# Products of constant tables on TensorE in six waits of a six-layer fp32 model block

## What is computed

```python
for layer in range(2):
    h = rms_norm(x, mix_pre_g[layer])
    m = mixer_ab(h, ...) if layer == 0 else mixer_cd(h, positions, ...)
    x = x + rms_norm(m, mix_post_g[layer])
    h = rms_norm(x, ffn_pre_g[layer])
    x = x + rms_norm(channel_mixer(h, ...), ffn_post_g[layer])
for l in range(2):
    x = hybrid_layer(x, l, ...)      # projections, four attention groups, output projection
return rms_norm_2(x, final_norm_g)
```

## Time and profile before

| | |
|---|---|
| median of 3 runs | 2828.29 us (2823.17 to 2831.08) |
| the profiled execution | 2837.55 us, span of the core 2835.7 us |
| mean granted TensorE clock | 0.99 |
| TensorE busy | 2749.1 us, 97% |
| VectorE, ScalarE, GpSimd busy | 1945.8 us (69%), 1379.4 us (49%), 518.3 us (18%) |
| read from HBM | 477.25 MB, 169 GB/s over the span |

### The profile page before, as it was taken

One profiled execution on the slowest core, in us unless ns is written; L12 is line 12 of the kernel. 1 busy time (PEld: TensorE's weight loads), 2 busy tenths in 40 slices (PEclk: granted clock), 3 DMA queues, 4 the chain that ended last, 5 costly groups with the idle time before them and its releaser, 6 DMA issues.

```text
span 2835.7 us, 50169 instructions
## 1 busy us (share of the span) xinstructions
PE 2749.1 (97%) x18314; PEld 2484.2 (88%) x18314; DVE 1945.8 (69%) x2757; ACT 1379.4 (49%) x1931; POOL 518.3 (18%) x487
## 2 busy tenths in 40 slices
PE   8999999999999999999999999999999999999998
PEld 8998988888888899988888888899878889987887
DVE  6675678777744787678777754676667766666775
ACT  5434555554544557555555444453445454344553
POOL 1150025444411000023444411000000020000001
PEclk9999999999999999999999999999999999999999
DMA  7455445555555455445555555444544555554454
GB/s 253 156 176 182 151 147 178 187 183 187 187 188 185 140 168 164 134 142 171 185 185 185 185 187 186 153 163 161 179 144 149 168 182 173 165 176 143 148 170 141
DMA packets 132569, 482.61 MB, mean 170 GB/s; under 512 B 15040, under 2 KB 15296, under 8 KB 132288
## 3 DMA queue, kind: packets, MB, share of 16 engines
q1 hardware_dynamic: 130608, 475.06, 51.1%
q10 hardware_dynamic: 1808, 5.39, 0.6%
HBM read 477.25 MB, written 2.10 MB: 169 GB/s over the span
## 4 chain that ended last, share of the span: by engine, by line
PE 90%; DVE 5%; ACT 2%; POOL 2%; issue 1%; DMA 0%; DVEq 0%; ACTq 0%; POOLq 0%
PE BANK L462 32%; PE BANK L457 28%; PE BANK L463 16%; PE BANK L478 8%; DVE WLO L1324 1%; PE BANK L839 1%; PE BANK L532 1%; ACT WHI L890 1%; PE BANK L469 1%; PE BANK L829 1%; PE BANK L849 0%; POOL M L2058 0%; DVE TM L1346 0%; PE BANK L676 0%; POOL M L2061 0%
## 5 line engine op out<-in xcount | busy, mean ns | idle before, releaser
L1324 DVE TENSOR_TENSOR WLO<-RING,WHI 128x1024 fp32r<-128x1024 f32 x902 | 1112.9, 1236 | 664.5 <-ACT WHI L890 657.7
L890 ACT ACTIVATE WHI<-RING 128x1024 fp32r<-128x1024 f32 x902 | 954.0, 1059 | 1144.4 <-PE BANK L463 636.2
L462 PE MATMUL BANK<-H,WHI 128*128 128x512 f32 x2560 | 917.8, 403 | 14.7 <-DVE H L1334 9.8
L457 PE MATMUL BANK<-H,WHI 128*128 128x256 f32 x4160 | 764.8, 286 | 22.3 <-DVE H L1334 19.0
L463 PE MATMUL BANK<-H,WLO 128*128 128x256 f32 x2560 | 719.8, 281 | 0.0
L457 PEld LDWEIGHTS BANK<-H,WHI 128*128 128x128 f32 x4160 | 653.2, 193 | 28.9 <-issue 23.2
L462 PEld LDWEIGHTS BANK<-H,WHI 128*128 128x128 f32 x2560 | 483.0, 189 | 136.0 <-issue 15.3
L457 PE MATMUL BANK<-H,WLO 128*128 128x256 f32 x2080 | 590.2, 284 | 0.0
L462 PE MATMUL BANK<-BIGR,WHI 128*128 128x512 f32 x1536 | 539.9, 396 | 3.4 <-DVE BIGR L1957 3.4
L463 PEld LDWEIGHTS BANK<-H,WLO 128*128 128x128 f32 x2560 | 485.5, 190 | 1.7 <-issue 1.0
L463 PE MATMUL BANK<-BIGR,WLO 128*128 128x256 f32 x1536 | 431.0, 281 | 0.0
(11 more groups left out here) (281 smaller groups left out, 2348.3 us busy)
## 6 DMA issues: line engine op xcount, KB each, us to landing
RING<-w SPq DMA_DIRECT2D x902, 512.0 KB, 3.3
X<-xT ACTq DMA_DIRECT2D x4, 512.0 KB, 9.9
outT<-M SPq DMA_DIRECT2D x3, 512.0 KB, 2.9
TB<-tab ACTq DMA_DIRECT2D x1, 1216.5 KB, 5.5
V<-vec ACTq DMA_DIRECT2D x1, 644.0 KB, 8.6
TM<-BIG ACTq DMA_DIRECT2D x16, 32.0 KB
TM<-BIG ACTq DMA_DIRECT2D x8, 64.0 KB
outT<-M SPq DMA_DIRECT2D x2, 256.0 KB, 3.2
```

The lines of the kernel that those rows point to most:

```text
L457: last = mm(bank[:, 0:T], wt[s][:, kk, :], x, start=start and n == 0, stop=stop and n == 2)
L462: mm(bank[:, :], WHI[s][:, kk, :], both, start=start, stop=False)
L890: A(WHI[at % SPLIT][:, :, :], RING[at % RAW][:, :].rearrange("p (k n) -> p k n", k=UB), ACT.Copy)\
L1324: TT(WLO[at % SPLIT][:, :, :], RING[at % RAW][:, :].rearrange("p (k n) -> p k n", k=UB), WHI[at % SPLIT][:, :, :].bitcast(f32), ALU.subtra ...
```

## The change

`occupy(bank, n)` issues `n` plain fp32 products of the table `ident` (stationary, 128x128) with the table `ones` (moving, 128x256) into the first 256 columns of a bank. Nobody reads the result; the next product into that bank starts afresh (`start=True`). It is called with 23 in `lead`, behind the wait for free banks and ahead of the waits for tiles, for the four leads that follow a post-norm (`u0` is 0 in the first lead of the program); with 15 ahead of the first wait for `lru_lo`; and with 14 at the head of `queries`, behind a wait for the bank, which the first product there has today as well.

```diff
+            def occupy(bank, n):
+                for _ in range(n):
+                    mm(bank[:, 0:T], ident, tcol("ones", T), start=True, stop=True)
@@ lead
                 pe.wait_ge(sem("bank_free"), o0)
+                if u0:
+                    occupy(banks[0], 23)
                 for h in range(UB):
                     pe.wait_ge(sem("lo_done"), u0 + h + 1)
@@ run, step
                             if r.src == "LRU" and isinstance(i, int) and i == 0 and j == 0:
+                                if k == 0:
+                                    occupy(BANK[o0 % BANKS], 15)
                                 pe.wait_ge(sem("lru_lo"), k + 1)
@@ queries
+                pe.wait_ge(sem("bank_free"), c["output"] - (BANKS - 1))
+                occupy(BANK[c["output"] % BANKS], 14)
                 pe.wait_ge(sem("normed_lo"), step_no(c, "norm_tiles", 6))
```

## The result

The change made the kernel slower: 2845.68 us (median of 13 runs, 2835.14 to 2856.97) against 2831.73 us (13 runs, 2817.46 to 2842.38), a ratio of 1.0056 with a 95% interval of 1.0039 to 1.0074, that is +15.9 us (11 to 21). The ratio is estimated from all runs; the two medians by themselves lie 14 us apart. Forecast were +14.3 us and a median of 2842.5 us, in a range of 2833 to 2852 us.

The account below looks back on a forecast made before the run. TensorE was taken to bound the kernel through its waits and clock; post-norms +13.0, queries +0.7 and LRU +0.6 us gave +14.3 us, added to the 2828.29 us median for 2842.5 us, range 2833 to 2852 us.

Parts of the forecast that it names:

- The price of a filler: At all six waits: each filling product is two passes of 0.216 us, so 0.43 us at full clock.
- first rival: At the six waits: a filler costs one pass, 0.216 us, leaving only the clock's gain; -9.5 us, 2819 us; 10%.
- The clock: Behind the first post-norm: fillers keep it up, sixteen products take 5.65 us instead of 7.34 us, 1.7 us comes back.
- third rival: At the six waits: fillers don't hold the clock; +12.5 us per post-norm, some +55 us in all, 2884 us; 5%.
- Nothing gives the time back: Behind the leads: TensorE's delay moves along whole, with no new wait and no later wait absorbing it.
- second rival: Second mixer and waits behind: DVE's and ACT's side work partly absorbs the overrun; +4 to +8 us, 2834 us; 12%.
- The sum: Over the six places: 13.0 us at post-norms, 0.7 us at queries, 0.6 us at LRU, together +14.3 us.
- six terms: Four post-norms +3.1, +3.2, +3.4 and +3.4 us, the queries +0.7 us, the LRU stage +0.6 us.
- the third post-norm: Lead after the third post-norm: its first L532 pair at 1276.5 us instead of 1273.07 us, +3.4 us.
- LRU term: In the first rival, at the LRU stage: products at full clock gain 1.7 us (4.62 - 2.9 us).

Follow-up runs that it names:

- double counts: The change with 46, 30 and 28 fillers in place of 23, 15 and 14: 2906.43 us against 2837.27 us for the kernel before, ratio 1.0248.
- second mixer alone: The change without fillers in the leads, keeping 15 at the LRU stage and 14 at the queries: one run, 2843.58 us.
- the kernel before once more: The unchanged kernel before, run again for a second trace: one run, 2831.93 us.
- post-norms alone: The change with its 23 fillers in each of the four leads only, none at the queries and the LRU stage: one run, 2843.97 us.
- fitted counts: The change with 12, 9 and 8 fillers in place of 23, 15 and 14: 2821.81 us against 2837.39 us for the kernel before, ratio 0.9955.
- half-width: The change with fillers of 128 columns in place of 256, same counts: 2821.42 us against 2837.27 us for the kernel before, ratio 0.9949.
- one-pass version: The change with fp32r fillers from a rounded table of ones, counts 42, 34 and 30: one run, 2826.88 us.
- six fillers: The change with six fillers in each of the four leads and none in the second mixer: one run, 2835.83 us.
- the last version: Half width plus 9 fillers ahead of the third post-norm's sums, 18 at LRU, 16 at queries: 2826.17 us against 2839.24 us for the kernel before, ratio 0.9960.

## Why the prediction was right

**The price of a filler**, 0.43 us from two readings of the squares, held: 0.216 us a pass in the change and 0.436 us a product from the double counts. It was the step that decided the sign, and the first rival (one pass per product) is refuted by the 242 records.

**The clock**, kept up by products that nobody reads: shown at 1.00 behind every wait that was filled whole, in plain fp32 and in fp32r, where it fell at each of the twelve post-norm waits left unfilled (two traces of before, second mixer alone). Behind the unfilled wait of the queries it stayed up in one trace, that of the kernel before once more. The third rival is refuted.

**Nothing gives the time back**: shown by the post-norms alone and by the double counts. The second rival is refuted, for the second mixer too.

**The sum**: +14.3 us predicted, +15.9 us (11 to 21) measured, +16.3 us in the six places of the profiled execution. Five of the six terms are right within 0.1 us. The sixth, the third post-norm, was +5.1 us in that execution and not +3.4 us: I had fillers at full clock there, and overlooked that TensorE waits 2.0 us for GpSimd just ahead of the sums, in which the change puts no filler and after which the clock can already fall. It did so in three of the six filled traces without an edit at that wait. How often it falls in the timed runs is not known, and their interval can't tell +14.6 us (clock up there) from +16.3 us, so the nearness of the two sums to the median is partly luck.

**The rival for a faster kernel** was priced at -9.5 us; the version that realises it gains 7.8 us in its places. Most of the difference is the LRU term, priced at 1.7 us and measured at 0.5 us, where I counted the clock's gain without asking whether the data for the fifth product would be there.

**What was misjudged** is the profiled execution: predicted at 2851.9 us, it was 2836.08 us. I had said that I take no term from the 9.3 us by which the profiled execution before lay above its median. The medians bore the sum out; the two single executions did not.

## What to carry to other kernels

A filled wait pays in one coin only, the clock behind it (0.5 to 1.6 us a place here against the first trace of before), and each filler that outlasts the wait costs its full length on a TensorE that bounds the kernel. So price a filler by the distance of two starts in the trace, times the passes that its type takes (count records, not instructions), fill the wait to its end but not beyond, and look for a short wait just ahead of it, after which the clock may already fall. Half a filling, six of twelve here, gained nothing at three of four places.

## What the runs showed of the hardware that was not expected

The wide products of a channel mixer have one of two prices, at a granted clock of 1.00 in both, 399 or 391 ns in the mean record (394 ns in one mixer each of the half-width and the one-pass version), and a mixer kept its price from the first half to the second. A cheap mixer is 9.4 to 9.7 us shorter. The change had two cheap ones in its trace, before none: 19.1 us, which hid the +16.3 us of the places and, with 1.5 us more behind the fourth post-norm, gave the shorter span. The second trace of before had one cheap mixer, as had fitted counts, post-norms alone, half width and the one-pass version; second mixer alone, double counts, six fillers and the last version had none. So the lower price needs no edit (the kernel before itself had both), and with one trace of most versions it stays open whether an edit shifts how often it comes. Some sets of times show steps of that size: 17 runs of before beside the last version have 2 at 2820 us, 2 at 2829 to 2831 us, and 13 at 2834 to 2843 us. The 13 runs of before beside the change show none; they spread from 2817 to 2842 us. What decides between the two prices was not tried and stays open.

The part behind the fourth post-norm scatters as well: from its first squares to the end it takes 1002.8 and 1006.3 us in the two traces of before, and 1000.3 to 1007.4 us over all traces. The timed gains of the versions whose fillers fit are larger than what their places gain (12.8, 14.5 and 11.4 us against 7.6, 7.8 and 7.8 us; for the first two the places' gain lies below the interval), and how much of the rest is the price of the mixers is not known. A change of some 10 us on this kernel can only be read from medians of many runs, or place by place.
